# An expert mixer in which ScalarE, tile by tile, turns each dot product into its weight

## What is computed

```python
def peer(xn, wq, k1, k2, u, v):          # 8 heads, 128 keys a side, 16 experts chosen per head
    q = (xn @ wq).reshape(B, S, HEADS, 2, HALF)
    s1, s2 = q[..., 0, :] @ k1.T, q[..., 1, :] @ k2.T
    t1, i1 = top_k(s1, 16); t2, i2 = top_k(s2, 16)
    cand_s = t1[..., :, None] + t2[..., None, :]
    cand_i = i1[..., :, None] * 128 + i2[..., None, :]
    top_s, pos = top_k(cand_s, 16)
    idx, gate = cand_i at pos, softmax(top_s)
    act = gelu(sum over d of x[t, d] * u[idx[t, e], d])
    out[t] = sum over e of gate[t, e] * act[t, e] * v[idx[t, e]]
```

## Time and profile before

| | |
|---|---|
| median of 3 runs | 3345.01 us (3344.4 to 3346.84) |
| the profiled execution | 3349.07 us, of it span 3346.9 |
| busy: TensorE, its weight load | 2863.7 us (86%), 1572.2 |
| busy: VectorE, ScalarE, GpSimd | 1982.2 (59%), 583.6 (17%), 727.3 us (22%) |
| TensorE's mean granted clock | 0.958 of full speed |
| read from memory | 1225.74 MB, mean 367 GB/s |
| gathers (software queue) | 1073.77 MB |

### The profile page before, as it was taken

One profiled execution on the slowest core, in us unless ns is written; L12 is line 12 of the kernel. 1 busy time (PEld: TensorE's weight loads), 2 busy tenths in 40 slices (PEclk: granted clock), 3 DMA queues, 4 the chain that ended last, 5 costly groups with the idle time before them and its releaser, 6 DMA issues.

```text
span 3346.9 us, 24916 instructions
## 1 busy us (share of the span) xinstructions
PE 2863.7 (86%) x8488; PEld 1572.2 (47%) x8488; DVE 1982.2 (59%) x3816; ACT 583.6 (17%) x1269; POOL 727.3 (22%) x571
## 2 busy tenths in 40 slices
PE   7999998888988777878879999888898787778777
PEld 6887864444443333333338786444454333333333
DVE  4454555555666666666665755555566666666665
ACT  4344311110111110010123531111111011000011
POOL 1000022322222222222210002222233222222221
PEclk9999999999998999899999999999999999999999
DMA  6544589999999999999985348999999999999998
GB/s 229 180 163 151 216 353 428 426 428 426 421 427 425 426 424 427 415 427 414 427 367 175 114 172 335 427 427 428 426 422 425 427 428 424 421 425 415 422 427 350
DMA packets 138749, 1229.45 MB, mean 367 GB/s; under 512 B 12928, under 2 KB 13696, under 8 KB 68096
## 3 DMA queue, kind: packets, MB, share of 16 engines
q0 software_dynamic: 73728, 1073.77, 75.8%
q1 hardware_dynamic: 61680, 147.99, 12.5%
q10 hardware_dynamic: 3216, 6.12, 0.5%
HBM read 1225.74 MB, written 2.10 MB: 367 GB/s over the span
## 4 chain that ended last, share of the span: by engine, by line
PE 49%; DMA 39%; DVE 7%; ACT 2%; issue 2%; POOL 0%; DVEq 0%; ACTq 0%; SPq 0%; POOLq 0%
DMA ring_sb<-in_peer_uv_dram,idx_cur 38%; PE bank L1211 25%; PE bank L936 15%; PE bank L983 5%; DVE ring_sb L1683 5%; ACT diag L760 1%; PE bank L995 1%; DVE w_parts L390 1%; ACT shared L756 0%; PE bank L1159 0%; ACT w_parts L384 0%; DMA ring_sb<-in_mlstm_w_out_dram 0%; DVE shared L1696 0%; PE bank L1018 0%; DVE shared L1692 0%
## 5 line engine op out<-in xcount | busy, mean ns | idle before, releaser
L1211 PE MATMUL bank<-ring_sb,diag 128*128 128x512 f32 x4096 | 1947.9, 631 | 439.6 <-ACT diag L760 439.6
L1683 DVE CUSTOM_DVE_ANT_0 ring_sb<-ring_sb,arena 128x2048 f32<-128x2048 f32 x512 | 1172.3, 2290 | 845.4 <-DMA ring_sb<-in_peer_uv_dram,idx_cur 845.4
L1211 PEld LDWEIGHTS bank<-ring_sb,diag 128*128 128x128 f32 x4096 | 805.5, 201 | 1540.6 <-issue 925.7
L551 POOL DMA_INDIRECT ring_sb<-in_peer_uv_dram,idx_cur x512 | 686.4, 1341 | 1872.1 <-PE bank L1211 1859.9
L936 PE MATMUL bank<-w_parts,actT_hi 128*128 128x512 f32 x1664 | 520.9, 394 | 9.3 <-DVE w_parts L390 7.7
L756 ACT ACTIVATE shared<-shared 128x2 f32<-128x2 f32 (+1 forms) x272 | 55.6, 205 | 2151.2 <-DVE shared L1692 2151.2
L390 DVE TENSOR_TENSOR w_parts<-ring_sb,w_parts 128x2048 fp32r<-128x2048 f32 x100 | 229.3, 2298 | 212.3 <-ACT w_parts L384 212.1
L936 PEld LDWEIGHTS bank<-w_parts,actT_hi 128*128 128x128 f32 x1664 | 310.2, 189 | 76.5 <-issue 12.5
L936 PE MATMUL bank<-w_parts,actT_lo 128*128 128x512 f32 x832 | 325.3, 391 | 0.0
L384 ACT CAST w_parts<-ring_sb 128x2048 fp32r<-128x2048 f32 x100 | 190.7, 1909 | 283.1 <-DMA ring_sb<-in_mlstm_w_in_dram 139.6
L760 ACT ACTIVATE diag<-const,shared 128x128 f32<-128x128 f32 x512 | 179.3, 394 | 90.1 <-DVE shared L1696 90.1
(11 more groups left out here) (169 smaller groups left out, 1090.7 us busy)
## 6 DMA issues: line engine op xcount, KB each, us to landing
ring_sb<-in_mlstm_w_in_dram SPq DMA_DIRECT2D x48, 1024.0 KB, 5.2
ring_sb<-in_attn_w_in_dram SPq DMA_DIRECT2D x20, 1024.0 KB, 5.2
ring_sb<-in_mlstm_w_out_dram SPq DMA_DIRECT2D x16, 1024.0 KB, 5.1
arena<-in_peer_wq_dram SPq DMA_DIRECT2D x16, 1024.0 KB, 11.4
ring_sb<-in_attn_w_out_dram SPq DMA_DIRECT2D x16, 1024.0 KB, 5.0
wq_more<-in_peer_wq_dram SPq DMA_DIRECT2D x12, 1024.0 KB, 15.8
ring_sb<-in_peer_uv_dram,idx_cur POOLq DMA_INDIRECT x512, 16.7
ring_sb<-in_peer_wq_dram SPq DMA_DIRECT2D x4, 1024.0 KB, 7.8
```

The lines of the kernel that those rows point to most:

```text
L551: nc.gpsimd.indirect_dma_start(out=uv_slot[at], out_offset=None, in_=uv_rows, in_offset=bass.IndirectOffsetOnAxis(ap=idx_cur[par][:, k:k + ...
L1211: last = mm(acc[n][:, :], diag[slot_of(gu, k)][:, :], v_slot[at][:, n * CH:(n + 1) * CH], start=False, stop=end and k == TOPK - 1, skip_gr ...
L1683: v.tensor_tensor_reduce(u_slot[at], u_slot[at], xn[b], 1.0, 0.0, ALU.mult, ALU.add, dots[:, k:k + 1]).then_inc(dot_done, 1)
```

## The change

ScalarE computes the whole weight, for one tile at a time in every unit. For tile k it takes the square of the dot (`e_x2`), the dot times the halved gate (`e_p`), then GELU_C * 0.044715 * square + GELU_C (`e_t`), tanh of the dot scaled by that (`e_th`), and e_th * e_p + e_p (`e_w`); then the diagonal as before. The operands scale and bias are columns of the core's memory in four of the five. Square, tanh and the two sums are chained by waits of ScalarE for its own last operation; `e_p` is issued without one behind the square. ScalarE waits for the gates once per unit (`gates_ready`) and for each dot (`dot_done`).

VectorE keeps the dots and the choice. The four small operations and the wait for tanh go, and so does the copy of the gates at the head of a unit with its wait: `chosen` writes the gates, halved, straight into one of two tiles, after a wait that the unit before the last has used its own. `finished_at` goes. The constants get 8 columns with GELU_C.

```diff
@@ ScalarE, in unit(u)
-                        tiles = finished_at(u, k)
-                        if tiles:
-                            c = slice(tiles[0], k + 1)
-                            act.wait_ge(tanh_in, gu * TOPK + k + 1)
-                            nc.scalar.activation(e_th[:, c], e_in[:, c], ACT.Tanh, scale=GELU_C).then_inc(tanh_out, len(tiles))
-                            act.wait_ge(w_ready, gu * TOPK + k + 1)
-                        for t in tiles:
-                            act.wait_ge(v_used, gu * TOPK + (t + 1))
-                            nc.scalar.activation(diag[slot_of(gu, t)][:, :], ident, ACT.Copy,
-                                                 scale=e_w[:, t:t + 1]).then_inc(diag_ready, 1)
+                        if k == 0:
+                            act.wait_ge(gates_ready, gu + 1)
+                        c = slice(k, k + 1)
+                        act.wait_ge(dot_done, gu * TOPK + k + 1)
+                        n = st.did(nc.scalar.activation(e_x2[:, c], dots[:, c], ACT.Square))
+                        st.did(nc.scalar.activation(e_p[:, c], gates[gu % 2][:, c], ACT.Copy, scale=dots[:, c]))
+                        st.need(n)
+                        n = st.did(nc.scalar.activation(e_t[:, c], e_x2[:, c], ACT.Identity, bias=gelu_c,
+                                                        scale=GELU_C * GELU_A))
+                        st.need(n)
+                        n = st.did(nc.scalar.activation(e_th[:, c], dots[:, c], ACT.Tanh, scale=e_t[:, c]))
+                        st.need(n)
+                        n = st.did(nc.scalar.activation(e_w[:, c], e_th[:, c], ACT.Identity, bias=e_p[:, c],
+                                                        scale=e_p[:, c]))
+                        act.wait_ge(v_used, gu * TOPK + (k + 1))
+                        st.need(n)
+                        nc.scalar.activation(diag[slot_of(gu, k)][:, :], ident, ACT.Copy,
+                                             scale=e_w[:, c]).then_inc(diag_ready, 1)
@@ VectorE, in chosen(gu)
-                did(v.tensor_scalar(gate_next[:, :], g_exp[:, :], g_rec[:, :], None, ALU.mult))
+                if gu > 1:
+                    dve.wait_ge(diag_ready, (gu - 1) * TOPK)
+                v.tensor_scalar(gates[gu % 2][:, :], g_exp[:, :], g_rec[:, :], 0.5, ALU.mult,
+                                ALU.mult).then_inc(gates_ready, 1)
@@ VectorE, in unit(u)
-                    need(st.n)
-                    if gu:
-                        dve.wait_ge(w_ready, gu * TOPK)
-                    need(did(v.tensor_scalar(gate_cur[:, :], gate_next[:, :], 0.5, None, ALU.mult)))
-
@@ VectorE, in expert(k), after the dot
-                        tiles = finished_at(u, k)
-                        if not tiles:
-                            return
-                        c = slice(tiles[0], k + 1)
-                        dve.wait_ge(dot_done, gu * TOPK + k + 1)
-                        need(did(v.scalar_tensor_tensor(out=e_t[:, c], in0=dots[:, c], scalar=GELU_A, in1=dots[:, c],
-                                                        op0=ALU.mult, op1=ALU.mult)))
-                        v.scalar_tensor_tensor(out=e_in[:, c], in0=e_t[:, c], scalar=1.0, in1=dots[:, c],
-                                               op0=ALU.add, op1=ALU.mult).then_inc(tanh_in, len(tiles))
-                        need(did(v.tensor_tensor(e_p[:, c], dots[:, c], gate_cur[:, c], ALU.mult)))
-                        dve.wait_ge(tanh_out, gu * TOPK + k + 1)
-                        v.scalar_tensor_tensor(out=e_w[:, c], in0=e_th[:, c], scalar=1.0, in1=e_p[:, c],
-                                               op0=ALU.add, op1=ALU.mult).then_inc(w_ready, len(tiles))
```

More of the change, by code:

```diff
@@ L31 @@
 C_SIN = C_COS + 256
-C_KEPT = C_SIN + 128
+C_GELU = C_SIN + 128
+C_KEPT = C_GELU + 8
 M_TRI, M_ONES, M_MASK = 0, 256, 384
@@ L67, in constants @@
     c[:, C_POW:C_POW + 8] = -0.5
+    c[:, C_GELU:C_GELU + 8] = GELU_C
     return c
@@ L144, in trunk_kernel @@
         iota = const[:, C_IOTA:C_IOTA + 16]
+        gelu_c = const[:, C_GELU:C_GELU + 1]
         xb = [x_sb[:, b * D:(b + 1) * D] for b in range(NB)]
@@ L207, in trunk_kernel @@
         bank_done = sem("bank_done")
-        tanh_in, tanh_out, w_ready, diag_ready = sem("tanh_in"), sem("tanh_out"), sem("w_ready"), sem("diag_ready")
+        gates_ready, diag_ready = sem("gates_ready"), sem("diag_ready")
         x_out, stored = sem("x_out"), sem("stored")
@@ L277, in trunk_kernel @@
         c_top, c_pos, c_ab, sel_if = tile(16), tile(16, U32), tile(32, U32), tile(32)
-        negmax, g_exp, g_sum, g_rec, gate_next, gate_cur = tile(1), tile(16), tile(1), tile(1), tile(16), tile(16)
+        negmax, g_exp, g_sum, g_rec = tile(1), tile(16), tile(1), tile(1)
+        gates = [tile(16), tile(16)]
         idx_next = sb("idx_next", 16, U32)
         idx_cur = [sb("idx_cur0", 16, U32), sb("idx_cur1", 16, U32)]
-        dots, e_x2, e_t, e_in, e_th, e_p, e_w = (tile(16) for i in range(7))
+        dots, e_x2, e_t, e_th, e_p, e_w = (tile(16) for i in range(6))
         diag = [sb(f"diag{i}", P) for i in range(NDIAG)]
@@ L398, in choice_at @@
             return (5, 7, 9) if u < HEADS else (3, 5, 7)
-        def finished_at(u, k):
-            if u == UNITS - 1:
-                return range(k, k + 1)
-            return range(k - 1, k + 1) if k % 2 else range(0)
         def queries_at(u):
```

## The result

The changed kernel takes **3314.04 us** in the median (3312.16 to 3314.77); the kernel before took 3345.57 beside it. The ratio is 0.9904 with a 95% interval of 0.9891 to 0.9917: faster by 1.0%, where I had written 3347.1 and "no change". The profiled execution took 3312.16 us with a span of 3310.3, against 3349.07 and 3346.9.

A forecast was written before the change was run, and what follows sets the result against it. The prediction took the expert-row gathers, paced by one trailing DMA engine, as the bound. Chain costs of 0.95 + 1.12 = +2.07 us on the median 3345.01 gave 3347.1 us, range 3340 to 3351.5.

The forecast's parts named there:

- What bounds the kernel: Both expert stages: gathers of expert rows set the pace, 4.90 us a tile; 413 of 512 dots waited, 845 us.
- One of the sixteen DMA engines trails: Expert-row gathers: one DMA engine also carries q8's code fetches, trails by a tile and never runs dry.
- the long step: Gather stream: one step of 5.88 us among plain 4.89, put down to a packet of q8, once per unit.
- VectorE loses four short operations ... so this gives 0: VectorE, every two tiles: four small operations and a wait go, but it waits for landings anyway; 0 us.
- The constants grow by 8 columns: 0: Constants ahead of the ring in core memory: 8 more columns were claimed to cost 0 us.
- The rates: Expert streams: 423 and 424 GB/s should stay; a rise to 428 over 1100 to 1700 would refute the trailing-engine reading.
- ScalarE's chain: Dot to first matmul, +0.56 us: +1.12 at both layer ends, +0.95 at layer 1's start, 0 at layer 0's.
- Single tiles in the steady stretch: Gather stream: slots come free some 3.6 us sooner, but gathers just queue longer, median near 21 us; 0 gain.
- TensorE's clock: Long stretches of the expert stages: granted clock rises from 0.93 and 0.94 to nearly 1.00, worth 0 us.
- Fuller queues: Rival, both expert stages: earlier slots bring 428 GB/s, 26 us won, 3321 us, or 3334 for half; 7%.
- ScalarE's code on the trailing engine: Rival, gather stream: 283 KB more code in 17 packets on the pace-setting engine, +17.7 us, 3363 to 3365; 5%.
- The table: Rival, ScalarE at every tile: Identity sharing no table with Tanh forces loads of 1.283 us, +1130 us; 1%.

The follow-up runs named there:

- e12: The changed kernel with eight waits per tile on TensorE, each on a count reached long ago; 3313.44 us, ratio to before 0.9896.
- e2: The changed kernel without the 8 columns, ScalarE writing its constant into a spare tile so the ring stays where it was; 3339.66 us, ratio to before 0.9976.
- e11: The changed kernel with a 128x2048 reduction on VectorE behind every fourth dot; 3315.14 us, ratio to before 0.9904.
- e3: The kernel before with 16 unused columns of constants, the ring starting 32 bytes past a multiple of 256; 3346.8 us, ratio 1.000.
- e14: The kernel before with eight waits per tile on ScalarE, each on a count reached long ago; 3347.27 us, ratio 1.0003.
- e1: The kernel before with 8 unused columns of constants, moving the ring's start to a multiple of 256 bytes; 3321.13 us, ratio 0.9921.
- e6: e2 with its tiles finished in pairs on ScalarE; 3338.74 us, ratio to before 0.9973.
- e16: The changed kernel once more, unchanged, run beside e13 and e14; 3313.68 us, ratio to before 0.9902.
- e10: The changed kernel with eight waits per tile on ScalarE, each on a count reached long ago; 3321.90 us, ratio to before 0.9921.
- e7: The kernel before with 8 unused columns just ahead of the ring and 56 just behind, moving the ring alone onto a multiple of 256 bytes; 3335.33 us, ratio 0.9962.
- e15: The changed kernel with 64 more unused columns of constants, the ring starting on a multiple of 16 KB; 3314.02 us.
- e4: The kernel before with 56 unused columns of constants, the ring on a multiple of 64 bytes but not of 256; 3342.95 us, ratio 0.9985.
- e9: The changed kernel with eight waits per tile on VectorE, each on a count reached long ago; 3327.61 us, ratio to before 0.9943.
- e13: The changed kernel with eight already satisfied waits per tile on both VectorE and ScalarE; 3327.77 us, ratio to before 0.9941.

## Why the prediction was wrong

**What bounds the kernel**: right, and it is so after the change. *One of the sixteen DMA engines trails*: right, the last raise of a gather comes 5.5 us behind the eighth and the one before it 1.2; but I gave the long step to the wrong queue. The argument was a count, one packet of q8 and two of q14 in 50 us with one long step. q14 carries the code of more than one engine, so two packets there could well be one each; the start of each packet against the start of the long dot would have told, as the fences above do. By e12 the cost of q8 is nothing.

**"VectorE loses four short operations ... so this gives 0"**: the failed step that is worth 7.6 us (e2). I covered their busy time, which e11 shows to be free indeed, and didn't ask for their code, although the next paragraph of my own text had code fetches setting the pace. Had I given the long step to VectorE, fetches at 1 in 25 tiles in place of 1 in 16 would have given (1/16 - 1/25) x 0.96 x 511 = -11.0 us for the streams; e2's streams are 11.1 us shorter. That they agree so closely is luck: the layer 1 stream took 1296.7 us in this execution of before and 1294.3 and 1294.1 in e3 and e14, whose step is the same. And the rule behind it, that ScalarE's new fetches cost nothing beside VectorE's, I could not have known from the rows of before.

**"The constants grow by 8 columns: 0"**: the failed step that is worth 26.1 us (e1). I took the columns for data of a few bytes and left out that all that is placed behind them moves. The rows of before could not have told the price, since they show one address; but that the 12 slots of the ring move by 32 bytes stood in the diff, and the bound should have had a term for it.

**The rates.** I wrote that a rise to 428 GB/s over 1100 to 1700 would show the reading wrong. It rose to 431, and e1 and e2 divide it: 428 with the address alone. The DMA share of 1.00 was the sign that idle queues were not what there was to win.

**ScalarE's chain**: right in place and size. 1.91 for 1.94 at the end, 1.86 for 1.90 and +0.88 for +0.95 at the start of layer 1, +0.49 for +0.56 from the last landing on. Its operations took 0.20 (Square), 0.28 (one operand from memory), 0.29 (Tanh) and 0.39 (two), for 0.20, 0.30, 0.30 and 0.39. The sum of +2.07 is inside the result; the terms that it doesn't know come to some 35 us the other way.

**Single tiles in the steady stretch**: 0, right. e6 against e2, the same work in pairs and singly, is 3338.74 against 3339.66. The gathers do just queue longer: from issue to landing the median is 20.9 us in e16, the changed kernel again (the profile of after gives none), for 16.7 before and a forecast of 21. **TensorE's clock**: right, 1.00 and 0.97 for 0.93 and 0.94, and worth nothing. **Busy times**: ScalarE +608 for some 700, VectorE -157 for some 170.

**The rivals.** *Fuller queues*: the time (3321 for its upper case) came near by luck. Its mechanism is refuted by e1, where no instruction differs and the stream is faster, and by e6, whose gathers take 16.3 us to landing, near those of before, in the same time as e2, which frees its slots singly as the change does. (Its 2525 us for both streams are 2591 by the dots' starts, which makes its 26 us 27.) *ScalarE's code on the trailing engine*: half right. Its code does slow the stream, by 7.9 us in e10, but only where it is the heaviest. In the change it is no heavier than what is left of VectorE's, and the landings show a second DMA engine trailing and not the first one further back. *The table*: Identity needed no load; ScalarE's row of Identity has a mean of 279 ns, no 1.283 us in it, as the page's group says (busy us, mean ns, idle before):

```profile
L757 ACT ACTIVATE shared<-shared,const 128x1 f32<-128x1 f32 x512 | 142.7, 279 | 0.0
```

**The range**, 3340.0 to 3351.5, left the result out by 26 us. Its ends came from the sum's own terms; neither failed step had a bound, since both stood at 0 without one.

## What to carry to other kernels

Where the bound is a stream of DMA, look at where its destination lies in the partition: here a start on a multiple of 256 bytes gave 0.8% for 8 unused columns, and an edit that grows a tensor ahead of it can win or lose that much. In such a kernel count instructions and not only busy time, engine by engine: of VectorE's and ScalarE's code the one that costs more per tile set the pace here, and more of the other cost nothing. TensorE's, the longest of all, cost nothing either, so which stream matters is a thing to try, with waits that hold nothing up. An edit of one line that changes no instruction, run by itself, is the first experiment to make when a time comes out beyond every term.

## What the runs showed of the hardware

- A gather of 128 rows of 16 KB took 4.85 us with the ring on a multiple of 256 bytes (e1, e7, e15) and 4.90 off it (before, e2, e3; e4 4.896): 432 against 428 GB/s.
- 4096 waits came to some 2048 instructions of two waits and 0.13 MB of code, 64 bytes each (e9, e10, e12). VectorE's and ScalarE's code comes in packets of 8 KB, TensorE's in 16 KB.
- Each 8 KB of VectorE's code made one tile's landing 0.96 us later (0.85 each in the time of e9), each 8 KB of ScalarE's 0.69 (0.49 each in e10), TensorE's 16 KB not measurably (-0.6 us for 8 packets more).
- The costs of two engines' code don't add up (e13: 3327.8, for 3327.6 with VectorE's alone; e14: 3347.3, for 3347.3 without). Sixteen raises of a gather's semaphore show one trailing before and two after.
- 282 us more of busy VectorE cost 1.1 us (e11).
